# First two supertiles channel-major, every transpose a DMA, and the mixer of supertile 3 inside a down projection

## What is computed

```python
h = rmsnorm(x, norm1_g);  z = h @ w_in            # 1024 -> [a 512 | u 512 | v 512]
a = z[:512];  u = gelu(z[512:1024]);  v = gelu(z[1024:])
d = trailing_mean(a, windows 2/4/8/16 in 4 groups) - a
pool = (d @ pool_w per group) * pool_scale         # and the last 15 rows of a are an output
gate = u * (W_s v + b)                             # per chunk of 128 tokens, 4 heads
x = x + concat(pool, gate) @ w_out
x = x + square(relu(rmsnorm(x, norm2_g) @ w_up)) @ w_down      # 1024 -> 4096 -> 1024
y = rmsnorm(x, normf_g)
```

## Time and profile before

| | us |
|---|---|
| median of 3 runs (lowest, highest) | 1323.41 (1321.47, 1346.49) |
| profiled execution | 1322.38 |
| its span, slowest core (4) | 1320.8 |
| spans of the 8 cores | 1311.8 to 1320.8 |
| TensorE busy in the span | 1242.6 (94%) |

### The profile page before, as it was taken

How to read it: one execution, slowest core, us unless ns; L and a number is a source line. 1 busy time by engine, 2 the same in 40 slices (tenths; PEclk the granted TensorE clock), 3 DMA queues, 4 the chain that set the end, 5 groups by cost and what they waited for, 6 DMA issues and landing times.

```text
span 1320.8 us, 19210 instructions; the slowest of 8 cores (1311.8 to 1320.8 us)
## 1 busy us (share of the span) xinstructions
PE 1242.6 (94%) x6733; PEld 657.7 (50%) x6800; DVE 543.4 (41%) x1147; ACT 405.4 (31%) x767; POOL 52.4 (4%) x98
## 2 busy tenths in 40 slices
PE   4678999999599999999999999999999999999995
PEld 2443554454354555455455455545545545554552
DVE  3653433445343444254354344425435434441412
ACT  4433341223432332142243234214224313430411
POOL 4000000001000000000000000000000000000000
PEclk9888999999799999999999999999999999999998
DMA  9992786645634953873794495377379439337751
GB/s 179 198 232 84 135 201 147 156 131 169 210 128 138 261 192 129 222 239 128 221 272 162 132 259 199 128 229 233 129 212 281 159 130 257 136 129 218 256 204 48
DMA packets 85918, 240.15 MB, mean 182 GB/s; under 512 B 52818, under 2 KB 53074, under 8 KB 63040
## 3 DMA queue, kind: packets, MB, share of 16 engines
q1 hardware_dynamic: 72464, 184.20, 44.1%
q0 software_dynamic: 13360, 54.72, 18.0%
HBM read 215.05 MB, written 34.43 MB: 189 GB/s over the span
## 4 chain that ended last, share of the span: by engine, by line
PE 90%; DMA 4%; DVE 2%; issue 2%; ACT 2%; POOL 0%; SPq 0%; DVEq 0%; ACTq 0%; POOLq 0%
PE ps L676 28%; PE ps L658 28%; PE ps L546 9%; PE ps L381 8%; PE ps L620 6%; PE ps L640 6%; PE ps L407 4%; DMA X<-xall 2%; DMA yall<-X 1%; DMA G1B<-norm_g 1%; PE ps L502 1%; DVE HB L305 1%; ACT JUNK L277 1%; PE ps L316 0%; DVE X L699 0%
## 5 line engine op out<-in xcount | busy, mean ns | idle before, releaser
L658 PE MATMUL ps<-H2T,RING 128*128 128x384 bf16 x2304 | 391.2, 327 | 12.5 <-ACT ST L662 12.0
L676 PE MATMUL ps<-RING,ST 128*128 128x512 bf16 x1692 | 371.1, 379 | 1.9
L658 PEld LDWEIGHTS ps<-H2T,RING 128*128 128x128 bf16 x2304 | 224.6, 98 | 162.1 <-issue 16.1
L676 PEld LDWEIGHTS ps<-RING,ST 128*128 128x128 bf16 x1728 | 169.0, 98 | 203.0
L277 ACT ACTIVATE JUNK<-X 128x1024 bf16<-128x1024 f32 x100 | 105.6, 1056 | 465.8 <-DVE SS L274 205.1
L662 ACT ACTIVATE ST<-ps 128x384 bf16<-128x384 f32 x288 | 136.0, 491 | 191.1 <-PE ps L658 191.1
L664 DVE TENSOR_TENSOR ST<-ST 128x384 bf16<-128x384 bf16 x288 | 96.0, 356 | 172.3 <-ACT ST L662 172.0
L381 PE MATMUL ps<-HT,WAU 128*128 128x384 bf16 (+1 forms) x704 | 117.9, 329 | 4.6 <-ACT HT L320 4.6
L681 DVE TENSOR_TENSOR X<-ps,X 128x512 f32<-128x512 f32 x54 | 37.4, 692 | 200.2 <-PE ps L676 200.2
L546 PE MATMUL ps<-WOUT,MIXT 128*128 128x512 bf16 x517 | 113.4, 379 | 0.6
L381 PEld LDWEIGHTS ps<-HT,WAU 128*128 128x128 bf16 x704 | 69.2, 99 | 51.4 <-issue 6.6
(11 more groups left out here) (83 smaller groups left out, 658.6 us busy)
## 6 DMA issues: line engine op xcount, KB each, us to landing
RING<-scr SPq DMA_DIRECT2D x144, 1024.0 KB, 6.2
RING<-w_mlp POOLq DMA_DIRECT2D x16, 1024.0 KB, 14.4
scr<-RING SPq DMA_DIRECT2D x16, 1024.0 KB, 11.3
X<-xall POOLq DMA_DIRECT2D x30, 512.0 KB, 5.9
yall<-X POOLq DMA_DIRECT2D x30, 512.0 KB, 9.5
WAU<-w_au POOLq DMA_DIRECT2D x4, 512.0 KB, 18.8
WOUT<-w_out POOLq DMA_DIRECT2D x2, 1024.0 KB, 26.5
X<-xall SPq DMA_DIRECT2D x3, 512.0 KB, 4.8
```

Of the source, the lines that this page charges most:

```text
L658: i_ = e.matmul(bank(ub)[:, 0:TOK], lhsT=RING[s][:, k, (m % 4) * 128:(m % 4 + 1) * 128], rhs=H2T[:, k, :], start=(k == 0), stop=(k == 7))
L676: i_ = e.matmul(bank(n)[:, :], lhsT=ST[:, kg * 8 + kk, n * 128:(n + 1) * 128], rhs=RING[s][:, kk, :], start=(kg == 0 and kk == 0), stop=(k ...
```

## The change

Supertiles 0 and 1 enter channel-major: two new inputs xt0 and xt1 hold their x transposed, XT0 and XT1 lie in slots of the ring, and the scales of norm 1 come from a product of a ones matrix with the squares summed over channel pairs, which gives each token's sum on all partitions. For supertile 0, HT is x times the norm's weight, and the scale is applied when the products are evacuated; for supertile 1 it is applied in eight DVE products into H2T. Supertile 1's mixer has buffers of its own, in ST, H2T and the ring (A1). All transposes are DMAs: those of norm 2 of supertiles 0 and 1 and of norm 1 of supertile 2 on ACT's queue, all others on SP's. In supertile 2's stage the mixer of supertile 3 moves: its norm 1 behind 18 UP groups, its input products behind 28, its pool and gating products and its output product among the down groups. The state outputs are written from A by DMA, and the 24 products go.

```diff
-        add("sp", lambda e: e.dma_start(out=X[0][:, 0, :], in_=xall[0:128, :]), writes=[("X", 0, 0)], dma="xld0sp_0")
+        for j in range(4):
+            add("sp", lambda e, j=j: e.dma_start(out=XT[0][:, 2 * j:2 * j + 2, :], in_=xt0[:, 2 * j:2 * j + 2, :]),
+                writes=[("XT0", j)], dma=f"xt0_{j}")
...
+        for j in range(4):
+            add("sp", lambda e, j=j: e.dma_start(out=XT[1][:, 2 * j:2 * j + 2, :], in_=xt1[:, 2 * j:2 * j + 2, :]),
+                reads=[("WAU", 0)], writes=[("XT1", j)], dma=f"xt1_{j}")
...
             add("pool", lambda e, m=m: e.dma_start(out=WAU[:, m:m + 2], in_=w_au[:, m:m + 2]),
-                reads=[("X", 0, 0)], writes=[("WAU", m), ("WAU", m + 1)], dma=f"wau{m}")
+                reads=[("XT0", 1)], writes=[("WAU", m), ("WAU", m + 1)], dma=f"wau{m}")
...
+        load_x(0, ("WV", 0))
+        load_x(1, ("WOUT", 0))
...
-        def norm_T(hb, dstT, dst_res, ncol0, np_=128):
+        def norm_T(hb, dstT, dst_res, ncol0, ch, q="sp"):
+            add(q, lambda e: e.dma_start_transpose(out=dstT[:, :, ncol0:ncol0 + 128], in_=HB[hb][:]),
+                reads=[("HB", hb)], writes=dst_res if isinstance(dst_res, list) else [dst_res], dma=ch)
...
+        def gen_first_x(s):
+            SQ = XT[0] if s == 0 else SQ1
...
+                add("act", lambda e, j=j: e.activation(out=SQ[:, 2 * j:2 * j + 2, :], in_=XT[s][:, 2 * j:2 * j + 2, :],
+                                                       func=AF.Square),
+                    reads=[] if s == 0 else [("XT1", j)], writes=sqk(j))
...
+        def gen_first_sum(s):
...
+            add("pe", lambda e: e.matmul(bank(fb)[:, 0:W], lhsT=ONES[:], rhs=SQ[:, 0, :], start=True, stop=True),
+                reads=["ONES", key], writes=[("BANK", fb)])
...
+        def gen_N2_T(i, n0=0, n1=NT):
+            q = "act" if i < 2 else "sp"
...
+                    norm_T(hbs[("2", i)][n], H2T1[:, :, n * 128:(n + 1) * 128], [("H2T1", n)] + [("ST", 16 + k) for k in range(8)], 0,
+                           f"tr2{q}1_{n}", q)
...
+                fin.append(add("sp", lambda e: e.dma_start(out=spp[:, :, :], in_=A[:, :, 257:272]), reads=Aall, dma="o_spp"))
...
+                held = []
+                if at < 4:
+                    held = [(f"XT{at // 2}", j) for j in range(4)]
+                elif at == 4:
+                    held = [("A1", g) for g in range(4)] + [("A1h", g) for g in range(4)]
...
-        gen_pair_UP(0, 0, 3, (0,))
         gen_WO_pe(1, squares=True)
-        gen_pair_UP(0, 3, 5, (0,))
+        gen_pair_UP(0, 0, 5, (0,))
...
+        gen_N2_T(1)
         gen_pair_DN(0, 0, 0)
-        gen_N2_T(1)
...
-                gen_N1_T(2)
+                gen_N1_T(2, "act")
...
             if i == 2:
+                gen_UP(i, 4, 18)
                 gen_N1_elem(3)
+                gen_N1_T(3)
+                gen_UP(i, 18, 28)
+                gen_WI_au(3)
...
```

More of the change, by code:

```diff
@@ L176, in build_nc @@
         JUNK = sb("JUNK", [128, D], BF16)
-        IDB = sb("IDB", [128, 128], BF16)
+        ONES = sb("ONES", [128, 128], F32)
+        G1T = sb("G1T", [128, 8], F32)
         POOLW = sb("POOLW", [128, 4, 128], BF16)
@@ new lines, in build_nc, with gen_warm, mm @@
+        RSB = [X[2][:, 0, 0:W0], X[2][:, 2, 0:TOK]]
+        VRB = [X[2][:, 0, 512:512 + W0], X[2][:, 2, 512:512 + TOK]]
+        NWB = [X[2][:, 1, 0:W0], X[2][:, 1, 512:512 + TOK]]
+        RSk = [("X", 2, 0), ("X", 2, 2)]
+        def gen_warm(cnt):
+            fb = next_front()
+            rhs = WSMTS[:].rearrange("p g c -> p (g c)")
+            def mm(e):
+                for _ in range(cnt):
+                    i_ = e.matmul(bank(fb)[:, :], lhsT=WSMTS[:, 0, :], rhs=rhs, start=True, stop=True)
+                return i_
+            add("pe", mm, reads=["WSMTS"], writes=[("BANK", fb)])
@@ L402, in gen_WI_v @@
+                if i == 0:
+                    late.append(evac)
+                else:
+                    evac()
+        late = []
+        def gen_WI_v(i, n0=0, n1=NT):
+            B = bufs(i)
+            for n in range(n0, n1):
                 fb = next_front()
@@ L444, in gen_PL @@
                         reads=["HSA"], writes=[("A", g) for g in range(4)])
+                Aall = [("A", g) for g in range(4)]
+                fin.append(add("sp", lambda e: e.dma_start(out=spp[:, :, :], in_=A[:, :, 257:272]), reads=Aall, dma="o_spp"))
+                for s in range(2):
+                    c0 = 337 + 80 * s
+                    fin.append(add("sp", lambda e, s=s, c0=c0: e.dma_start(out=sps[:, s], in_=A[:, :, c0:c0 + 15]),
+                                   reads=Aall, dma=f"o_sps{s}"))
             for g in range(4):
-                src = A[:, g, :]
-                src_res = [("A", g), ("Ah", g)]
+                src = B.A[:, g, :]
+                src_res = [B.Ak(g), B.Ahk(g)]
                 cur = None
@@ L533, in gen_PG, with gen_WO_pe @@
                 p()
-        def gen_WO_pe(i, squares=False):
+        def gen_WO_pe(i, squares=False, n0=0, n1=NT):
             b = i % NXB
-            if squares:
+            B = bufs(i)
+            if squares and n0 == 0:
                 norm_memset("2")
-            MIXall = [("MIXT", k) for k in range(8)]
-            for n in range(NT):
+            MIXall = [B.MIXk(k) for k in range(8)]
+            for n in range(n0, n1):
                 for hh in range(2):
@@ new lines, in build_nc @@
+                pieces = gen_PG_pieces(3)
+                gen_DN(i, 0, 0)
+                for k in range(4):
+                    pieces[k]()
+                gen_DN(i, 0, 1)
+                for k in range(4, 8):
+                    pieces[k]()
+                gen_DN(i, 0, 2)
+                gen_WO_pe(3)
+            else:
+                gen_UP(i, 4, 8)
+                if nxt:
+                    gen_WI_au(i + 1)
+                    gen_WI_v(i + 1)
+                    gen_PL(i + 1)
+                gen_UP(i, 8, 18)
+                pieces = gen_PG_pieces(i + 1) if nxt else []
+                for k in range(8):
+                    if pieces:
+                        pieces[k]()
+                    gen_UP(i, 18 + k, 19 + k)
+                gen_UP(i, 26, 30)
+                if nxt:
+                    gen_WO_pe(i + 1)
+                    gen_N2_elem(i + 1)
+                gen_UP(i, 30, 32)
+                gen_DN(i, 0, 0)
+                gen_DN(i, 0, 1)
+                gen_DN(i, 0, 2)
+                if nxt:
+                    gen_N2_T(i + 1)
```

394 lines of the change are left out of this document (206 added, 188 removed).

## The result

The changed kernel takes 1401.24 us (median), where the kernel before takes 1322.44: the ratio is 1.060, interval 1.0579 to 1.0621. The prediction was 1322.6 with a range of 1296 to 1341. The profiled execution's slowest core (2) has a span of 1398.9 us, 78.1 more than before. The medians are over all executions, a few of which ran slower on one die; the ratios are of undisturbed ones, and so are the times of e1 to e7, e9, e11 and e13, from one execution each. Each experiment stands beside the kernel before on its own chip.

A forecast was written before the change was run, and what follows sets the result against it. TensorE was taken as the bound, busy 109.98 of 110.30 us in the steady stage. 1322.4 + 9.1 + 2.8 + 7.5 - 13.9 - 5.3 = 1322.6 us, eight in ten from 1296 to 1341.

The forecast's parts named there:

- N1(2) on ACT's queue: Pair stage: supertile 2's norm 1 transposes share DMA with casts and stores, stalling WI_au(2) by +7.5 us (0 to 21).
- Rival A: Transposes pass freely beside casts: first UP at 114.5, no stall for supertile 2's norm 1, 1312.6 us; chance 0.25.
- Rival B: Transposes on ACT's queue wait until casts and stores run empty, and hold ACT: 1344 us; chance 0.17.
- the point of decision: Pair stage: the slower rival applies once supertile 2's norm 1 transposes land over 10 us late.
- The front, up to the first UP: From the start through supertiles 0 and 1's chain: first UP at 117 (107 to 124), making the front +9.1 us.
- The two gates: Front: first weight load waits for all XT1 slices; ACT's square of XT0 slice 1 waits for all WAU loads.
- (b) to (f): Front: chain from WAU's issue about 15 and landing about 31, through scales and DVE passes, to third HB at 110.2.
- (g): Front's end: transposes on ACT's queue, 114.5 at best; with DMA draining about 117 to 121, 117 taken for first UP.
- From the first UP to DN(0,0,1): Stretch to the second down group: 37.2 us left of 53.1, plus a +2.8 wait for supertile 1's norm 2 transposes.
- Supertile 2's stage: New mixer order removes 18.0 us, including the 12.0 Relu wait, against new waits: -13.9 (-10 to -18).
- Last supertile: The 24 state products leave TensorE for three small DMAs on SP: -5.3 us (-3 to -5.3).
- Rivals C and D: C: shorter front, first UP at 99, 1294.6 us, chance 0.15. D: supertile 2's stall remains, 1334.6 us, chance 0.05.

The follow-up runs named there:

- e1: The changed kernel with the three transposes of norm 1 of supertile 2 back on TensorE: 1330.07 us beside 1321.99 of the kernel before.
- e7: The kernel of e6 with the second and fourth casting ring loads no longer waiting for the one before them: 1332.98 us beside 1329.91 of the kernel before.
- e9: The kernel before with plain loads of x for supertiles 5 to 10 moved in the program ahead of SP's transposes, yet still issued early: 1330.58 us.
- e11: The kernel before with plain loads of x for supertiles 5 to 10 waiting for a ring load, to run beside SP's transposes; no total time given.
- e13: The changed kernel with each casting load from the sixth on split into eight: 1354.17 us beside 1332.03 of the kernel before.
- e6: The kernel of e1 with separate names for the two new gates, removing two accidental waits in the front: 1334.05 us beside 1329.91 of the kernel before.
- e8: The kernel before with only supertile 2's new stage order, its transposes on SP, and state outputs by DMA: 1314.07 us, ratio 0.9939.
- e10: The kernel of e7 with the transposes of norm 2 of supertiles 0 and 1 also by TensorE: 1315.77 us, ratio 0.9947 to the kernel before.
- e3: The changed kernel with casting loads from the sixth on waiting until the three transposes of norm 1 of supertile 2 have landed: 1336.81 us.
- e2: The changed kernel with the three DMA transposes of norm 1 of supertile 2 issued from SP instead of ACT: 1377.87 us.

## Why the prediction was wrong

**N1(2) on ACT's queue: the step that failed.** The step said "the two queues share packet for packet as far as rows show it, 720 against 573" and let the 192 pieces of an engine end when the queued work does, 34.0 us after, for +7.5 with a bound of 21. The two counts are no share: they are the loads and stores that were issued in that stretch, 5.24 and 4.18 MB. Packets do take turns one for one where queues are full (189, 189 and 186 in e7), but the step then added durations that each kind of traffic had without the other, where it had to count turns: 192 turns at one cast packet each, 0.76 us by the earlier trace rows, are 146 us. Measured are 198 steps in 103 us, an engine that has casts left holding all the others; that is 59.1 + 8.7 + 4.5 of wait, of which the cause of the 8.7 is open, and 79.7 with the cold clock. The bounds were worked out from the same sum, so the true value lay outside all of them. I had written that no row showed transposes beside casts; the bound from above should have been open there, and it was the one place of the sum with no nearest row.

The Trainium skill's rule that I weighed ("DMA: Bandwidth & Descriptors", section "Queues, rings and completion order": a whole packet of one ring before the next) would have given 20 us at most, by my estimate of some 15 turns; the trace has 50 to 82 from issue to landing. On the taking of turns the trace agrees (e7, one for one); their size differs, one piece a turn here and not 9 to 17, so 198 turns. On that size the measurement decides.

**Rival A** falls with that. **Rival B** had the direction and the place (the point of decision, N1(2) over 10 us late, was passed), and Relus did stand behind ACT's hold (4.5 on the slowest core, up to 18.8 on others). Its mechanism was another: the transposes did not wait for the casts to run empty, they slowed them, and 1344 was 57 short.

**The front, up to the first UP.** Forecast 117, measured 128.56, outside the bounds of 107 to 124. The two gates were there as read: WAU was issued at 16.98 (15), the first product, which needs it, began at 37.85 after a wait of 29.8. (b) to (f) were mis-sized together by 12: the first of the transposes of norm 2 was issued at 119.58 where the walk had 107.7. WAU let ACT go on at 34.95 (31); the reciprocal in each scale chain took 2.65 and 2.55 where a pass was put at 0.65, so the scales of supertile 1 were there at 62.1 (53); the gating passes waited for TensorE until 87.27 (77.6). (g) was close, 9.0 from the first issue to UP against 9.3, but by luck: on other cores these transposes took up to 11.7 to land, and UP waited up to 10.4 for them, beside 5.25 on this core. e6 confirms the walk's claim that the chain hangs on the gates (18 us), and shows what it lacked: a chain that ends sooner meets the casts.

**From the first UP to DN(0,0,1).** 34.1 where 37.2 + 2.8 were forecast. The 37.2 kept the cold clock of before (granted 0.85 in that stretch, 0.94 now). The wait for the three transposes of N2(1) that wait for each other was 2.2 against 2.8: right, and no cast was beside them (3.0 to 3.1 to land).

**Supertile 2's stage: right, in part by luck.** -14.8 against -13.9; the wait of WI_au(3) was 1.87 where I took 3.3 (0.4 to 5.6). But e8 shows that it hung on where the loads of x lie, which the step did not ask. Where the pair stage is not late, the wait is 3.7 (e1), 4.3 (e10) and 7.6 (e8), and the stage 11.2, 10.8 and 7.0 shorter than before.

**Last supertile: right.** -5.4 against -5.3, no new wait for the first pool product.

**Rivals C and D.** The front was not shorter, and the stall did not come back.

## What to carry to other kernels

Before a transpose goes from TensorE to a DMA, ask what other DMA traffic is under way in the stretch where it will run, and measure the two together: in these runs a transpose took one step per packet of its neighbour, so casting loads were the worst (0.63 us a packet), stores (0.32) and plain loads cost some, and alone it landed in 3.2 us. While weights stream in through casting loads, leave the transposes on TensorE, or hold the casts until they have landed; shorter cast packets help. And read the waits of a name-based order after each change: a load that "reads" a name to be late gives that name a reader, for which its next writer waits.

## What the runs showed of the hardware that I had not expected

A DMA transpose of 256 KB lands 3.2 us after issue alone (e3), 9.9 to 16.5 in the medians of six stages beside plain fp32 loads (e11), 23.0 in the median beside casts of short packets (e13), and 50 to 82 beside casts of long ones and stores, on the slowest core of the changed kernel (31.7 to 82.0 over all cores); from SP's queue it is 17.0 to 57.7 over all cores (e2). In that state the 16 engines are shown as busy and move 26 GB/s: about 16 pieces of 256 bytes start together, and the next group starts one cast packet later. TensorE's granted clock in the wait was 0.54 in 206 to 225 and 0.50 in 225 to 245, the lower of its two levels, with TensorE idle since 205.6; WI_au(2), at the end of it, took 12.71 us instead of 10.56.
